# Column sums of five norms: VectorE adds seven of the eight tiles, TensorE multiplies that sum and the last tile by ones

## The reference, cut to what matters

```python
def rms_norm(x, g):
    xf = x.astype(jnp.float32)
    y = xf * lax.rsqrt(jnp.mean(xf * xf, axis=-1, keepdims=True) + EPS)
    return (y * g.astype(jnp.float32)).astype(x.dtype)

def layer_norm(x, g=None, b=None):
    x32 = x.astype(jnp.float32)
    mu = jnp.mean(x32, axis=-1, keepdims=True)
    xc = x32 - mu
    y = xc * lax.rsqrt(jnp.mean(xc * xc, axis=-1, keepdims=True) + LN_EPS)
...
    # first block, each of two layers
    h = rms_norm(x, g_mix[l]) * (1.0 + sc_m[:, None]) + sh_m[:, None]
...
    x = x + gt_m[:, None] * (merged @ w_out[l])
    h2 = rms_norm(x, g_ffn[l]) * (1.0 + sc_f[:, None]) + sh_f[:, None]
...
    x = x + gt_f[:, None] * ((jax.nn.silu(gate) * up) @ w_down[l])
...
    # second block, one layer
    h = layer_norm(x) * (1.0 + sc_m) + sh_m
...
    x = layer_norm(DEEPNORM_ALPHA * x + g_m * mix, ln_mix_g[l], ln_mix_b[l])
```

## Time and profile before

| | |
|---|---|
| median of three runs | 3343.92 us (3341.67 to 3350.64) |
| span of the profiled execution | 3345.6 us |
| TensorE busy with matmuls | 3109.0 us, 93% |
| VectorE busy | 1703.4 us, 51% |
| ScalarE busy | 1259.6 us, 38% |
| GpSimd busy | 1092.6 us, 33% |
| granted TensorE clock, mean | 0.968 of full speed |

### The profile page before, as it was taken

How to read it: one execution, slowest core, us unless ns; L and a number is a source line. 1 busy time by engine, 2 the same in 40 slices (tenths; PEclk the granted TensorE clock), 3 DMA queues, 4 the chain that set the end, 5 groups by cost and what they waited for, 6 DMA issues and landing times.

```text
span 3345.6 us, 36876 instructions
## 1 busy us (share of the span) xinstructions
PE 3109.0 (93%) x13938; PEld 2315.4 (69%) x13938; DVE 1703.4 (51%) x2799; ACT 1259.6 (38%) x1877; POOL 1092.6 (33%) x538
## 2 busy tenths in 40 slices
PE   5997999999989889999998998999999997999997
PEld 3664777887756567788775776877777864666664
DVE  6687663222057857422103355755766136666664
ACT  3455224223245542332323443223334224554552
POOL 1241333444423314344342553534444421000001
PEclk9998999999999989999999998999999998999998
DMA  5110553443321136374332224634432324899993
GB/s 216 57 57 26 189 191 99 145 126 93 106 88 57 38 110 216 109 293 140 95 107 80 90 77 137 212 102 120 122 114 65 96 72 162 351 372 376 382 378 124
DMA packets 192665, 501.26 MB, mean 150 GB/s; under 512 B 20144, under 2 KB 102192, under 8 KB 176384
## 3 DMA queue, kind: packets, MB, share of 16 engines
q1 hardware_dynamic: 168816, 415.15, 36.4%
q0 software_dynamic: 13200, 49.32, 3.8%
q10 hardware_dynamic: 10496, 34.71, 3.1%
HBM read 463.83 MB, written 35.29 MB: 149 GB/s over the span
## 4 chain that ended last, share of the span: by engine, by line
PE 76%; DVE 13%; ACT 4%; DMA 3%; issue 3%; ACTq 1%; POOL 0%; DVEq 0%; POOLq 0%; SPq 0%
PE banks L699 19%; PE banks L701 18%; PE banks L700 18%; PE banks L1311 4%; PE banks L1291 2%; PE banks L1292 2%; PE banks L1293 2%; PE banks L756 2%; DMA ring<-in_w_all 2%; PE banks L791 1%; PE banks L781 1%; PE banks L802 1%; DVE arena L2192 1%; DVE abuf L2043 1%; DVE abuf L2134 1%
## 5 line engine op out<-in xcount | busy, mean ns | idle before, releaser
L2756 POOL TENSOR_TENSOR w_lo<-ring,w_hi 128x1024 fp32r<-128x1024 f32 (+1 forms) x379 | 915.9, 2419 | 1505.9 <-ACT w_hi L1424 1505.8
L700 PE MATMUL banks<-h_lo,w_hi 128*128 128x512 f32 x2104 | 834.2, 396 | 0.0
L1424 ACT ACTIVATE w_hi<-ring 128x1024 fp32r<-128x1024 f32 (+1 forms) x379 | 392.9, 1038 | 608.9 <-DMA ring<-in_w_all 518.7
L699 PE MATMUL banks<-hx_hi,w_hi 128*128 128x512 f32 (+2 forms) x1400 | 582.7, 416 | 34.7 <-DVE h_lo L1995 11.7
L701 PE MATMUL banks<-hx_hi,w_lo 128*128 128x512 f32 (+2 forms) x1400 | 554.5, 396 | 0.0
L700 PEld LDWEIGHTS banks<-h_lo,w_hi 128*128 128x128 f32 x2104 | 400.8, 190 | 94.2 <-issue 8.4
L699 PEld LDWEIGHTS banks<-hx_hi,w_hi 128*128 128x128 f32 (+2 forms) x1400 | 267.5, 191 | 134.6 <-issue 58.3
L701 PEld LDWEIGHTS banks<-hx_hi,w_lo 128*128 128x128 f32 (+2 forms) x1400 | 266.8, 191 | 60.2 <-issue 0.2
L699 PE MATMUL banks<-hf_hi,w_hi 128*128 128x512 f32 x704 | 278.0, 395 | 4.0 <-DVE h_lo L1995 4.0
L701 PE MATMUL banks<-hf_hi,w_lo 128*128 128x512 f32 x704 | 279.3, 397 | 0.0
L2292 DVE TENSOR_TENSOR arena<-sgs,banks 128x512 f32<-128x512 f32 x44 | 30.2, 687 | 346.6 <-PE banks L701 346.6
(11 more groups left out here) (400 smaller groups left out, 5346.1 us busy)
## 6 DMA issues: line engine op xcount, KB each, us to landing
ring<-in_w_all SPq DMA_DIRECT2D x356, 512.0 KB, 3.9
arena<-in_w_all SPq DMA_DIRECT2D x26, 2048.0 KB, 11.1
ring<-in_w_all SPq DMA_DIRECT2D x46, 1024.0 KB, 6.1
arena<-in_w_all SPq DMA_DIRECT2D x80, 512.0 KB, 5.4
arena<-in_w_all SPq DMA_DIRECT2D x25, 1024.0 KB, 7.8
abuf<-in_w_all SPq DMA_DIRECT2D x48, 512.0 KB, 5.1
h<-in_w_all SPq DMA_DIRECT2D x23, 1024.0 KB, 7.5
routed<-abuf POOLq DMA_DIRECT2D x1, 12288.0 KB, 50.6
```

Of the source, the lines that this page charges most:

```text
L699: pe.matmul(bank[0:m, :], upper, hi, start=first, stop=False)
L700: pe.matmul(bank[0:m, :], upper, lo, start=False, stop=False)
L1424: act.activation(w_hi[s][:, 0:n], raw_w[s][:, 0:n], ACT.Copy).then_inc(w_upper, 1)
L2756: pool.tensor_tensor(w_lo[s][:, 0:n], raw_w[s][:, 0:n], w_hi[s][:, 0:n], ALU.subtract)\
```

## The change

VectorE keeps a running sum of the tiles. After it has made `x[t]` for t = 2 to 7 it adds one tile to the sum (`added`, six additions of 128x512 per norm), so that at the end one tile holds the sum of tiles 0 to 6. TensorE then does two column sums in place of eight, both after product 7: that of the running sum, for which it waits on VectorE's sixth addition, and that of tile 7 (`two_sums`). The running sum is kept in the tiles of squares themselves, or for ln1 and ln2 in `squares` and `h`. All six column sums that stood between the products are gone. The rest of the kernel is the same.

```diff
--- before.py
+++ after.py
@@ -757,6 +757,14 @@
                 if k == KC - 1:
                     mm.then_inc(aux_full, 1)
 
+            def two_sums(a, added, last, all_added, last_made):
+
+                aux_for(a)
+                pe.wait_ge(sem("added"), all_added)
+                pe.matmul(aux, ones, added, start=True, stop=False)
+                last_made()
+                pe.matmul(aux, ones, last, start=False, stop=True).then_inc(aux_full, 1)
+
             def aux_product(a, lhsT, rhs, m=P, n=SEQ):
                 aux_for(a)
                 pe.matmul(aux[0:m, 0:n], lhsT, rhs, start=True, stop=True).then_inc(aux_full, 1)
@@ -995,13 +1003,10 @@
                     product(p + 3, [(u + 2, 4 * P, chunks_of(attb_hi, attb_lo, range(4)))])
                 side_by_side(at("out", "lin"), at("out", "unit"),
                              chunks_of(mg_hi, mg_lo, range(KC), lambda k: (sem("m_split"), layer * KC + k + 1)), apart=6)
-                for t in range(1, 8):
-                    if t > 1:
-                        product(at("out", "lin", t), [(at("out", "unit", t), 0, chunks_of(mg_hi, mg_lo, range(KC)))])
-
-                    for k in ([t - 1] if t in range(1, 7) else [6, 7] if t == 7 else []):
-                        column_sum(at("norm2", "aux"), lambda k: h[:, k, :], k,
-                                   lambda k: pe.wait_ge(sem("x_squared"), layer * (2 * KC) + KC + k + 1))
+                for t in range(2, 8):
+                    product(at("out", "lin", t), [(at("out", "unit", t), 0, chunks_of(mg_hi, mg_lo, range(KC)))])
+                two_sums(at("norm2", "aux"), h[:, 6, :], h[:, 7, :], 12 * layer + 6,
+                         lambda: pe.wait_ge(sem("x_squared"), (layer + 1) * (2 * KC)))
                 keep_going(6)
                 side_by_side(at("gu", "lin"), at("gu", "unit"),
                              chunks_of(hf_hi, h_lo, range(KC), lambda k: (sem("h_split"), layer * (2 * KC) + KC + k + 1)))
@@ -1017,13 +1022,12 @@
                         pieces.append((at("down", "unit", t) + n, 0, chunks))
                         k += count
                     product(at("down", "lin", t), pieces)
-                    for k in ([t - 1] if t in range(1, 7) else [6, 7] if t == 7 else []):
-                        if layer + 1 < LAYERS:
-                            column_sum(LAYER.at("norm1", "aux", 0, layer + 1), lambda k: squares[:, k, :], k,
-                                       lambda k: pe.wait_ge(sem("x_squared"), (layer + 1) * (2 * KC) + k + 1))
-                        else:
-                            column_sum(SECOND.at("ln1", "aux"), lambda k: x[:, k, :], k,
-                                       lambda k: taken(pe, at("down", "lin", k)))
+                if layer + 1 < LAYERS:
+                    two_sums(LAYER.at("norm1", "aux", 0, layer + 1), squares[:, 6, :], squares[:, 7, :], 12 * layer + 12,
+                             lambda: pe.wait_ge(sem("x_squared"), (layer + 1) * (2 * KC) + KC))
+                else:
+                    two_sums(SECOND.at("ln1", "aux"), squares[:, 6, :], x[:, 7, :], 12 * layer + 12,
+                             lambda: taken(pe, at("down", "lin", 7)))
 
 
             at = lambda stage, counter, turn=0: SECOND.at(stage, counter, turn)
@@ -1208,11 +1212,9 @@
                 product(p + 1, [(u + 1, 0, chunks[:8]), (u + 2, 0, chunks[8:])])
             side_by_side(at("out", "lin"), at("out", "unit"),
                          chunks_of(mg2_hi, mg2_lo, range(KC), lambda k: (sem("m_split"), LAYERS * KC + k + 1)), apart=6)
-            for t in range(1, 8):
-                if t > 1:
-                    product(at("out", "lin", t), [(at("out", "unit", t), 0, chunks_of(mg2_hi, mg2_lo, range(KC)))])
-                for k in ([t - 1] if t < 7 else [6, 7]):
-                    column_sum(at("ln2", "aux"), lambda k: x[:, k, :], k, lambda k: pe.wait_ge(sem("x_mixed"), k + 1))
+            for t in range(2, 8):
+                product(at("out", "lin", t), [(at("out", "unit", t), 0, chunks_of(mg2_hi, mg2_lo, range(KC)))])
+            two_sums(at("ln2", "aux"), h[:, 6, :], x[:, 7, :], 12 * LAYERS + 6, lambda: pe.wait_ge(sem("x_mixed"), KC))
             squares_summed("ln2", 1)
             keep_going(5)
             for k in range(KC):
@@ -2278,9 +2280,18 @@
                     produced(dve, p)
                     STT(x[:, k, :], lin[p % 2], gate_col, x[:, k, :], MUL, ADD).then_inc(lin_free[p % 2], 1)
 
+                def added(dst, first, second, count):
+
+                    if count % 6 != 1:
+                        dve.wait_ge(sem("added"), count - 1)
+                    TT(dst, first, second, ADD).then_inc(sem("added"), 1)
+
                 dve.wait_ge(sem("x_back"), 16 * layer + 16)
                 for t in range(8):
                     residual(at("out", "lin", t), t, mod[:, 16 + t:17 + t])
+                    if t >= 2:
+                        dve.wait_ge(sem("x_squared"), layer * (2 * KC) + KC + t)
+                        added(h[:, t - 1, :], h[:, t - 2, :], h[:, t - 1, :], 12 * layer + t - 1)
                 scaled_tiles(h, x, at("norm2", "aux"), lower_h(hf_hi, (layer * 2 + 1) * KC))
 
                 dve.wait_ge(sem("c_ready"), layer + 2)
@@ -2300,6 +2311,12 @@
                     TT(hid_lo[:, k, :], hid[:, k, :], hid_hi[k], SUB).then_inc(sem("hid_split"), 1)
                 for t in range(8):
                     residual(at("down", "lin", t), t, mod[:, 40 + t:41 + t])
+                    if t >= 2 and layer + 1 < LAYERS:
+                        dve.wait_ge(sem("x_squared"), (layer + 1) * (2 * KC) + t)
+                        added(squares[:, t - 1, :], squares[:, t - 2, :], squares[:, t - 1, :], 12 * layer + 6 + t - 1)
+                    elif t >= 2:
+                        taken(dve, at("down", "lin", t - 1))
+                        added(squares[:, t - 1, :], x[:, 0, :] if t == 2 else squares[:, t - 2, :], x[:, t - 1, :], 12 * layer + 6 + t - 1)
                 mine.restart()
 
 
@@ -2548,6 +2565,8 @@
                 TS(tmp[:, :], lin[p % 2], mod[:, 16 + t:17 + t], None, MUL).then_inc(lin_free[p % 2], 1)
                 taken(dve, p)
                 tell(STT(x[:, t, :], x[:, t, :], ALPHA, tmp[:, :], MUL, ADD), sem("x_mixed"))
+                if t >= 2:
+                    added(h[:, t - 1, :], x[:, 0, :] if t == 2 else h[:, t - 2, :], x[:, t - 1, :], 12 * LAYERS + t - 1)
             layer_norm("ln2", 1, x)
             dve.wait_ge(sem("x_affine"), KC)
             layer_norm("ln3", 2, h)
```

## The result

| | before | after |
|---|---|---|
| median of six runs each | 3344.82 us (3340.01 to 3350.64) | 3323.07 us (3321.08 to 3328.51) |
| span of the profiled execution | 3345.6 us | 3322.8 us |
| TensorE busy | 3109.0 us | 3079.5 us |
| VectorE busy | 1703.4 us | 1722.2 us |

What follows compares the result with a forecast made beforehand. TensorE's chain, 76% of the span, was taken as the bound. 28.0 us gross less 5.0 paid is 23.0, less 1.6 for the clock is 21.4: 3343.9 to 3322.5 us, range 3313 to 3334.

Steps and rivals of the forecast that it cites:

- What goes: Column sums removed from between products in "down" and "out" at five norms: 28.0 us gross saved.
- What comes, beside other work: Five of six additions per norm fall into VectorE's waits of 5.60 us or more and cost nothing.
- norm2, 0.8 us: At norm2, twice: the last sum starts 0.8 us later, behind the sixth addition; GpSimd is idle then.
- norm1, 0: At norm1 of layer 1: GpSimd holds the sixth addition, but ScalarE's root waits for the store anyway; cost 0.
- the cover: At norm1: ScalarE's wait for the store of `x` hides later sums, with 0.2 us to spare; beyond it, lateness is paid.
- ln1, 1.8 us: At ln1: GpSimd holds the sixth addition, mean read 2.49 us later, store covers 0.66; 1.8 us paid.
- VectorE first at ln1: Rival: sixth addition at ln1 gets in ahead of GpSimd, the 1.8 us are not paid: 3320.7 us; chance 0.15.
- ln2, 1.6 us: At ln2: the addition comes after both instructions of `x[7]`, sums start at 2743.2 and 2744.05, not 2742.42; 1.6 us paid.
- I count one more of them: TensorE's longer waits after product 7 bring one more low-clock stretch, 1.6 us; bounds one fewer and four more.
- held everywhere: Rival: GpSimd's splits meet the sixth addition at norm2 and ln2 too, three times up to 2.4 us: 3329.7; chance 0.08.
- the ring: Rival: the weights' ring becomes the bound, removed sums return as waits for weights: 3345.7, no change; chance 0.04.
- slower, by the clock: Rival: longer waits lower the clock through the following double product, say 7 us at each of five norms: 3356; chance 0.03.

Runs made afterwards that it cites:

- the removal alone: Kernel before without the column sums of tiles 0 to 5 and without any addition, mean taken over tiles 6 and 7 alone: 3314.57 us, ratio 0.9904.
- the run with GpSimd behind it: Changed kernel, but GpSimd's split of the weights at norm1 and ln1 waits for the sixth addition: 3315.78 us, ratio 0.9931.

## Why the prediction was right

The time, 3323.07, lies 0.6 us from 3322.5. The mechanism was right: what the sums cost, that the additions are free beside other work, and that the sixth one is paid. That the number was met so closely is luck: what is paid behind the last residual was put 2.4 us too small (6.6 with the clock, 9.0 measured), and 3.2 us came from outside the changed places. By the steps:

- **"What goes", 28.0 us: right**, 28.6 in the changed kernel, and the same in the removal alone. The first sum of "out" gave 1.6 to 1.7 us (residuals 1 and 2 were 7.51 us apart before and 5.91 after), as worked out from the bank's release. The other fifteen in "out" cost 0.91 us each, not 0.86; that is most of the difference.
- **"What comes, beside other work", nothing: right.** The additions alone cost nothing that can be measured. GpSimd stretched additions in "down" to as much as 1.78 us, and the 12 us and more of waiting there took it.
- **norm2, 0.8 us: right**, 0.86.
- **norm1, 0: 0.43 us.** GpSimd began 0.49 us ahead of the addition, not 0.11, so the addition ended 2.13 us behind the start of the residual, half a microsecond sooner than forecast. The clock used that up: from the first sum to the root it took (1.05 + 2.01) - (0.86 + 1.16) = 1.0 us, more than the store covered, and the root waited for TensorE. The prediction had named the cover and what its loss costs.
- **ln1, 1.8 us: mis-sized, 3.5.** The held addition was right (2.70 us; the run with GpSimd behind it has 0.68), and so, nearly, was the forecast that the store covers only 0.66 (4.10 us lost at the mean, 3.51 at the first square: 0.59). The term lacked the 1.7 us of clock. The rival *VectorE first at ln1* did not happen, but the run with GpSimd behind shows its price: ln1 gains 5.3 us over before, about what the rival gave it (5.1), and 3.7 more than the change; the squares took 8.80 us in both.
- **ln2, 1.6 us: mis-sized, 3.4.** The addition and sums stand within 0.1 us of the forecast; the clock took 1.6 more.
- **"I count one more of them", 1.6 us: the step that failed.** The prediction listed waits of 1.4, 2.7, 3.6 and 2.6 us and counted one low stretch for all of them, with no row that told how long a wait draws one. The waits came out at 1.54, 2.31, 3.55 and 2.50 us, and three of them drew one: those of 2.50 and 3.55 us had the low clock over both sums, that of 2.31 over part, that of 1.54 none. In the five places the time at low clock rose from 6.8 us to 16.6. It cost 1.7 us at ln1, 1.6 at ln2 and 0.4 at norm1, some 3.7 of the 9.0 us paid.
- **What made it good again was luck**: 3.2 us less outside the places. Where 23.0 - 1.6 = 21.4 was forecast, the places gave 19.6 and the rest 3.2, 22.8 of the span. The changed kernel's second measurement, 15 us less than before, does not hold 21.4 in its interval; it lies in the forecast's range all the same.

GpSimd started 0.19 us ahead at ln1, and the addition took 2.70 us, ending 0.55 us after GpSimd did. That agrees with the rule of the Trainium skill, "SBUF — State Buffer", section "SBUF: two separate sides", that whoever starts first keeps the shared port to the end. The run with GpSimd behind the addition doesn't test the other order, since a semaphore held GpSimd back there. The kernel before has that order at another place (timelines of DVE and POOL):

```profile
186.23 0.69 DVE L2133 SCALAR_TENSOR_TENSOR roots<-tmp,roots 128x512 f32<-128x512 f32 x1
...
186.51 2.67 POOL L2756 TENSOR_TENSOR w_lo<-ring,w_hi 128x1024 fp32r<-128x1024 f32 x1 [4.75 <-ACT w_hi L1424]
```

VectorE, 0.28 us ahead, took its usual 0.69 us, and GpSimd's split 2.67 where the shortest of its size took 2.34.

Of the rivals, *held everywhere* fell (at norm2 and ln2 the sixth addition took 0.68 and 0.69 us), *the ring* fell (idle 0.0 over 138 matmuls, residuals 15.22 us apart), and *slower, by the clock* had the mechanism but not the length: the low stretch lay over the two sums, 1.7 us, and not over the double product.

## What to carry to other kernels

Taking work out of a full TensorE stream paid here at its spacing in that stream, and vector work in VectorE's waits was free; but the last link, the one that needs the last tile, should not get a step longer. Here one more sum on TensorE (tile 6 by itself) was cheaper than the sixth addition, because it ran while TensorE had to wait anyway. Where an edit opens a wait of the size seen here (2.3 to 3.6 us) ahead of a product on the path, price that product at the low clock, once for each place, and try products of constants in the gap.

## What the runs showed of the hardware

- Behind waits of 2.31, 2.50 and 3.55 us the granted clock was 0.64, 0.51 and 0.51 over the sums. Two filling products (1.7 us) ahead of the wait left it at 1.00 and took 3.4 us off ln2, though TensorE did more. A wait of 1.54 us (norm2) had no such cost.
- Sixteen matmuls of ln1's squares took 7.10 us in one run and 8.80 in another of the same kernel, and up to 10.13 in others: where the low clock falls differs there from run to run. The squares of ln2 were regular, 8.80 us in all eight profiles without a filling ahead of the sums or the squares and 7.10 or 7.11 in the three with one. What decides that was not found.
- At ln1 GpSimd's hold of 2.0 us on the addition cost 3.7 us, since TensorE's longer wait had a low clock behind it.
